# Gate and up products of a SwiGLU layer as seven half products instead of eight, in two token groups

## The reference, cut to what matters

```
def swiglu(hn, w_gate_up, w_down):
    gate, up = jnp.split(hn @ w_gate_up, 2, axis=-1)
    return (jax.nn.silu(gate) * up) @ w_down

        h = h + memory_cross_attention(hn, mem, ...)      # ends with  o @ w_xo
        hn = rmsnorm(h, norm_ffn_g[l])
        h = h + swiglu(hn, w_gate_up[l], w_down[l])
    return rmsnorm(h, norm_final_g)
```

## Time and profile before

| what | us |
|---|---|
| median of 3 runs (2631.83 to 2634.83) | 2632.27 |
| the profiled execution | 2631.12 |
| its span | 2629.4 |
| PE busy in the span | 2526.4 |
| DVE / ACT / POOL busy | 1284.7 / 546.5 / 283.7 |

### The profile page before, as it was taken

One profiled execution on the slowest core, in us unless ns is written; L12 is line 12 of the kernel. 1 busy time (PEld: TensorE's weight loads), 2 busy tenths in 40 slices (PEclk: granted clock), 3 DMA queues, 4 the chain that ended last, 5 costly groups with the idle time before them and its releaser, 6 DMA issues.

```text
span 2629.4 us, 31047 instructions
## 1 busy us (share of the span) xinstructions
PE 2526.4 (96%) x11282; PEld 2056.1 (78%) x11282; DVE 1284.7 (49%) x2113; ACT 546.5 (21%) x733; POOL 283.7 (11%) x238
## 2 busy tenths in 40 slices
PE   6899999799999999999999999999999999999994
PEld 4688887688888788888768888888888888888883
DVE  6634553368880784352442554434434434433437
ACT  5301110322221432130331321111111111111122
POOL 3278870000000220000000000000000000000001
PEclk9999999999999999999999999999999999999997
DMA  5432227532226642222310000000000000000002
GB/s 191 133 117 99 86 74 156 146 122 80 80 80 168 200 175 76 84 96 80 104 57 32 32 33 32 33 32 32 32 32 32 32 32 32 32 32 32 32 16 96
DMA packets 87288, 201.27 MB, mean 77 GB/s; under 512 B 12608, under 2 KB 41792, under 8 KB 87232
## 3 DMA queue, kind: packets, MB, share of 16 engines
q1 hardware_dynamic: 83872, 189.01, 22.2%
q0 software_dynamic: 3360, 11.54, 1.4%
HBM read 148.64 MB, written 53.97 MB: 77 GB/s over the span
## 4 chain that ended last, share of the span: by engine, by line
PE 90%; DVE 3%; DMA 2%; issue 2%; POOL 1%; ACT 1%; SPq 0%; DVEq 0%; POOLq 0%; ACTq 0%
PE bank L616 28%; PE bank L617 28%; PE bank L618 28%; PE bank L893 2%; PE bank L839 1%; PE bank L870 1%; DMA BBL<-scratch_BB 1%; POOL ACC L515 1%; DMA scratch_CO<-COS 1%; DVE HR L1774 1%; PE bank L836 0%; DVE ACC L1613 0%; PE bank L713 0%; PE bank L882 0%; PE bank L781 0%
## 5 line engine op out<-in xcount | busy, mean ns | idle before, releaser
L616 PE MATMUL bank<-XN,WLO 128*128 128x512 f32 x2400 | 935.5, 390 | 3.1 <-DVE XN L1711 1.7
L617 PE MATMUL bank<-XN,WHI 128*128 128x512 f32 x2400 | 933.8, 389 | 0.0
L618 PE MATMUL bank<-XN,WHI 128*128 128x512 f32 x2400 | 933.7, 389 | 0.0
L616 PEld LDWEIGHTS bank<-XN,WLO 128*128 128x128 f32 x2400 | 450.4, 188 | 98.8 <-issue 5.1
L617 PEld LDWEIGHTS bank<-XN,WHI 128*128 128x128 f32 x2400 | 450.5, 188 | 94.2 <-issue 1.0
L618 PEld LDWEIGHTS bank<-XN,WHI 128*128 128x128 f32 x2400 | 450.4, 188 | 93.9
L948 ACT ACTIVATE WHI<-WR 128x1024 fp32r<-128x1024 f32 x150 | 157.7, 1051 | 603.1 <-PE bank L618 537.3
L1243 DVE TENSOR_TENSOR WLO<-WR,WHI 128x1024 fp32r<-128x1024 f32 x150 | 197.8, 1319 | 126.3 <-ACT WHI L948 118.0
L1758 DVE TENSOR_TENSOR HR<-bank,HR 128x512 f32<-128x512 f32 x264 | 181.8, 691 | 126.9 <-PE bank L618 125.0
L616 PE MATMUL bank<-AF,WLO 128*128 128x512 f32 x528 | 208.2, 394 | 0.7 <-DVE HR L1758 0.7
L617 PE MATMUL bank<-AF,WHI 128*128 128x512 f32 x528 | 208.0, 394 | 0.0
(11 more groups left out here) (200 smaller groups left out, 2526.4 us busy)
## 6 DMA issues: line engine op xcount, KB each, us to landing
WR<-W_all SPq DMA_DIRECT2D x150, 512.0 KB, 3.3
scratch_G<-GS SPq DMA_DIRECT2D x16, 768.0 KB, 3.8
XS<-xT SPq DMA_DIRECT2D x8, 768.0 KB, 4.9
scratch_CO<-COS SPq DMA_DIRECT2D x8, 768.0 KB, 4.1
COL<-scratch_CO SPq DMA_DIRECT2D x8, 768.0 KB, 4.3
G2L<-scratch_G SPq DMA_DIRECT2D x8, 768.0 KB, 5.8
G1L<-scratch_G SPq DMA_DIRECT2D x8, 768.0 KB, 7.2
XR<-xT SPq DMA_DIRECT2D x8, 768.0 KB, 4.3
```

Of the source, the lines that this page charges most:

```text
L616: pe_mm(out, w[1], x[0], start=first, stop=False)
L617: pe_mm(out, w[0], x[1], start=False, stop=False)
L618: return pe_mm(out, w[0], x[0], start=False, stop=last)
```

## The change

The eight half products of a gate/up step (gate and up, two halves of the 1024 features, two halves of the tokens) become seven (Strassen's scheme in the form with four combinations on either side). Tokens are taken in two groups of 768 (`GRP`), each of two halves of 384 (`HB`); the whole feed-forward part runs once for each group, with all weights read twice. A step is one D_FF tile of one group: 7 products of 4 k tiles x 3 matmuls of 384 columns. A chunk's down part is 4 entries of 24 matmuls of 384 columns. A step's activations are gated during the next step (`gated`, `gated_lo`), so the down part of a chunk stands after the first step of the next one.

The weights now pass through an entry ring: an entry is 128x512, its high part made by ACT (`EH`), its low part by DVE (`EL`), six entries (`RINGF`) ahead of PE. Three of a step's seven entries come straight from the loaded slots (`RAW`, three buffers), four are combinations that GpSimd makes into `SW` (`combine`). The combinations of the inputs (`XF`, `XH`, `XL`) are made once for each group; as silu stands behind sums of products, the norm's reciprocal is now multiplied into the inputs. `XN` is no longer used after xo; `AF` moves from `w0` + 48 KB to `base` + 84 KB (`base` is 2048; `w0` is 133312, that is 64 bytes above a multiple of 128). Group 0's final norm is computed in group 1's first steps, its output written late in group 1's last chunks, and stored by SP after the last weight load.

```
+PRODUCTS = ((0, B11), (1, T2), (0, B21), (1, T3), (2, T1), (3, T4), (2, B22))
+    def operand(kind, rg, ru):
+        gate, up = RAW[rg % RAWS], RAW[ru % RAWS]
+        return (gate[:, 0:BLK], SW[1][:], gate[:, BLK:], SW[2][:], SW[0][:], up[:, BLK:], SW[3][:])[kind]
 # SP
-        with loop(nc.sync, (NSLOT - 2 - SLOT0["ffn"]) // 2) as i:
-            for par in range(2):
-                weights(SLOT0["ffn"] + par + 2, par, i)
+            def pair(i):
+                raw_load(r + 4, f0 + 6 + 6 * i, n + 7 + 18 * i)
+                raw_load(r + 5, f0 + 7 + 6 * i, n + 10 + 18 * i, G_STEPS * g + 2 + 2 * i)
+                raw_load(r + 6, f0 + 4 + 6 * i, n + 13 + 18 * i)
+                raw_load(r + 7, f0 + 5 + 6 * i, n + PAIR0 + 3 + 18 * i, G_STEPS * g + 3 + 2 * i)
+                raw_load(r + 8, f0 + 8 + 6 * i, n + PAIR0 + 6 + 18 * i)
+                raw_load(r + 9, f0 + 9 + 6 * i, n + PAIR0 + 9 + 18 * i)
 # GpSimd
+        def combine(s, rg, ru, i, read):
+            pool.wait_ge(S(f"raw{ru % RAWS}"), raw_count(ru, i))
+            if read is not None:
+                pool.wait_ge(S("entry_lo"), read)
+            nc.gpsimd.tensor_tensor(SW[0][:], up[:, 0:BLK], up[:, BLK:], ALU.add)
+            nc.gpsimd.tensor_tensor(SW[1][:], SW[0][:], gate[:, 0:BLK], ALU.subtract)
+            nc.gpsimd.tensor_tensor(SW[2][:], gate[:, 0:BLK], up[:, 0:BLK], ALU.subtract)
+            nc.gpsimd.tensor_tensor(SW[3][:], gate[:, BLK:], SW[1][:], ALU.subtract)
+            def pair(i):
+                combine(s + 2 + 2 * i, r + 4, r + 5, i, n + PAIR0 + 18 * i)
+                combine(s + 3 + 2 * i, r + 8, r + 9, i, n + PAIR0 + 7 + 18 * i)
 # PE
+        def ffn_step(n, p, s, g, first=False):
+            for j, (bk, op) in enumerate(PRODUCTS):
+                pe.wait_ge(S("entry_lo"), n + j + 1)
+                if first:
+                    pe.wait_ge(S("x_ready"), 7 * g + j + 1)
+                if j == 2:
+                    pe.wait_ge(S("first_kept"), s + 1)
+                if j == 3:
+                    pe.wait_ge(S("summed"), 5 * s + 1)
+                if j == 6:
+                    pe.wait_ge(S("summed"), 5 * s + 3)
+                for a in range(HT):
+                    last = product(PS[bk][:, 0:HB], ...)
+                last.then_inc(S("products"), 1)
+            def pair(i):
+                ffn_step(n + PAIR0 + 18 * i, 2, s + 2 + 2 * i, g)
+                down(n + PAIR0 + 7 + 18 * i, 3, d + i)
+                ffn_step(n + PAIR0 + 11 + 18 * i, 1, s + 3 + 2 * i, g)
 # ACT, in a step
+            for j in range(7):
+                act.wait_ge(S("products"), 7 * s + j + 1)
+                if j == 0:
+                    copy(S1T[:], PS[0][:, 0:HB]).then_inc(S("first_kept"), 1)
+                if j == 2:
+                    nc.scalar.activation(SG1[:], PS[0][:, 0:HB], ACT.Silu)
+                if j == 0:
+                    next_hi(6, n + 6, q, s, rg, ru, i)
+                elif follow == "S":
+                    next_hi(j - 1, n + 6 + j, q, s + 1, ng, nu, i)
+                elif j < 5:
+                    down_hi(j - 1, n + 6 + j, q, rd, i)
+                if j in (1, 2) and not fresh:
+                    act_hi(s - 1, 1 - odd, j - 1)
+                if j == 6:
+                    act.wait_ge(S("summed"), 5 * s + 5)
+                    nc.scalar.activation(SG2[:], G2T[:], ACT.Silu)
 # DVE, in a step
+            for j in range(7):
+                if j == 1: with_first(U2T, 1, S1T, ...)
+                if j == 3: with_first(U3T, 1, S1T, ...)
+                if j == 4: with_first(UP2, 2, U3T, ...)
+                if j == 5: with_first(UP1, 3, U3T, ...)
+                if j == 6: with_first(G2T, 2, U2T, ...)
+                (entry_lo of entry n + 6 + j)
+                if j in (1, 2) and not fresh:
+                    gated(s - 1, j - 1)
+                if j == 3 and not fresh:
+                    gated_lo(s - 1, 1 - odd, 0)
+                    gated_lo(s - 1, 1 - odd, 1)
 # DVE, ahead of group 0 (ahead of group 1 the same order, mixed with down_add of the last chunk)
-        residual("xo", 2, False)
+        norm_reciprocal(0)
+        norm_reciprocal(1)
+        normed(0, B11, 0, 0).then_inc(S("x_made"), 1)
+        then(normed(0, T3, 0, 1))
+        tt(xf(T1), xf(T3), xf(B11), ALU.subtract)
+        x_lo(0, 0)
+        then(normed(0, B22, 1, 1))
+        entry_lo(1, ...); entry_lo(2, ...)
+        V.tensor_tensor(xf(T2), xf(B22), xf(T1), ALU.subtract).then_inc(S("x_made"), 1)
+        normed(0, B21, 1, 0).then_inc(S("x_made"), 1)
+        tt(xf(T4), xf(B21), xf(T2), ALU.subtract)
+        x_lo(0, 1)
+        x_lo(0, 2)
+        V.tensor_tensor(xf(T3), xf(B22), xf(T3), ALU.subtract).then_inc(S("x_made"), 1)
+        entry_lo(3, ...); x_lo(0, 3); entry_lo(4, ...); x_lo(0, 4); entry_lo(5, ...); x_lo(0, 5); x_lo(0, 6)
+        norm_reciprocal(2)
+                if last and g:
+                    for k in range(KT):   # group 0's output, 8 operations of 768 columns
+                        V.scalar_tensor_tensor(out=h, in0=h, scalar=gains[:, 4, k:k + 1], in1=RB[:, 0:GRP], ...)
...
```

More of the change, by code:

```diff
@@ L945, in _ @@
+        final_sums(1)
     @block.scalar
@@ new lines, in down, with x_hi, final_square @@
+        def down(n, p, s, d, ng, nu, i):
+            for m in range(4):
+                act.wait_ge(S("down_made"), 16 * d + 4 * m + 4)
+                next_hi(2 + m, n + 6 + m, (p + 6 + m) % RINGF, s, ng, nu, i)
+        def x_hi(g, j):
+            act.wait_ge(S("x_made"), 4 * g + min(j + 1, 4))
+            copy(XH[j][:], XF[j][:]).then_inc(S("x_high"), 1)
+        def final_square(g, k, out):
+            act.wait_ge(S("down_added"), 16 * (CHUNKS * (g + 1) - 1) + 2 * (k + 1))
+            if g == 0 and k:
+                act.wait_ge(S("final_added"), k)
+            nc.scalar.activation(out[:], HR[:, k, g * GRP:(g + 1) * GRP], ACT.Square).then_inc(S("final_squares"), 1)
@@ L1763, in _, with xo_pair @@
[L1763 to L1771 removed]
+        then(V.memset(ACC2[:], 0.0))
+        def xo_pair(i):
+            for par in range(2):
+                j = 2 * i + par
+                if not (isinstance(i, int) and i == 3 and par):
+                    lo(SLOT0["xo"] + par + 1, 2 * i)
+                for b in range(NB):
+                    h = one(HR, j)[:, blk(b)]
+                    V.tensor_tensor(h, take(RES0["xo"] + NB * par + b, i, 2 * NB), h, ALU.add).then_inc(evac, 1)
+                if par or not (isinstance(i, int) and i == 0):
+                    add_squares(2, j - 1, SQ2[:, 1 - par, :])
@@ new lines, in down_add, with down, normed @@
+        def down_add(d, g, m):
+            for r in range(4):
+                dve.wait_ge(S("down_made"), 16 * d + 4 * m + r + 1)
+                h = HR[:, 2 * m + r // 2, gcol(g, r % 2)]
+                V.tensor_tensor(h, PS[4 + r][:, 0:HB], h, ALU.add).then_inc(S("down_added"), 1)
+        def down(n, p, s, d, g, ng, nu, i):
+            for m in range(4):
+                down_add(d, g, m)
+                next_lo(2 + m, n + 6 + m, (p + 6 + m) % RINGF, s, ng, nu, i)
+        def normed(g, out, half, b):
+            for a in range(HT):
+                k = half * HT + a
+                last = V.scalar_tensor_tensor(out=XF[out][:, a, :], in0=HR[:, k, gcol(g, b)],
+                                              scalar=gains[:, 3, k:k + 1], in1=RB[:, gcol(g, b)],
+                                              op0=ALU.mult, op1=ALU.mult)
+            return last
```

516 lines of the change are left out of this document (379 added, 137 removed).

## The result

The changed kernel takes 2669.93 us (median; 2667.18 to 2670.76) where the kernel before took 2632.05 beside it: a ratio of 1.0141, 95% interval 1.0123 to 1.0158, so it is slower by 38 us, where I had forecast 11. The direction came out as forecast and the time lies inside the range, but the change is more than three times the forecast one: the forecast was 27 us too low, because the stalls of TensorE cost more than I had priced them at.

The account below looks back on a forecast made before the run. PE, busy 96% of the span, was taken as the bound: 1495.9 + 1006.6 + 42 + 22 + 5 + 4.3 + 1.7 + 40 + 23.9 = 2641.4 us of span, so 2643 forecast, range 2600 to 2682.

Parts of the forecast that it names:

- Distance of matmuls (173.3 ns): Feed-forward part on PE: each 384-column matmul costs 173.3 ns, 5808 of them 1006.6 us, a gain of 81.
- the columns' case (170.0): Rival, feed-forward matmuls: the surplus goes by columns, 170.0 ns each, minus 19 us, 2624; chance 0.13.
- the weight loads (188): Rival, feed-forward matmuls: a weight load of 188 ns bounds each one, 1091.9 us, no gain, 2728; chance 0.03.
- AF's surplus: Down matmuls: AF's 20.0 ns surplus is 6.7 larger from starting 64 bytes off; aligned like XN, down costs 173.3.
- GpSimd and DVE take turns: Steps beside combine: their times add, delaying a step's third sum; PE stalls 2.0 in 20 steps, 40 us (to 52).
- The rival in which the four operations fall into DVE's waits for ACT: Inside steps: GpSimd costs little, a step loses 0.3 instead of 2.0, 34 us go, 2609; chance 0.23.
- Between the groups, 22 + 5 + 2: PE waits 22 us for activations and group 1's inputs, 5 for group 0's norm, about 2 for a step's stall.
- Output operations, 4.3: Group 0's eight 768-column output operations on DVE stand before a down part; PE waits 4.3 us.
- Way in 42: From xo to the first steps: inputs need the norm first, step 0 ends at 1552.2 not 1510.5, 42 us lost.
- tail 23.9: Behind the last matmul: 23.9 us instead of 42.1, a gain of 18, as half the tokens are already out.
- the last down part: End of group 1: PE waits 1.7 us again for the activations gated only then.
- late chain: Rival, inside steps: handovers take 0.2 more, all 44 steps lose 0.8 more, plus 35 us, 2678; chance 0.14.

Follow-up runs that it names:

- b1_aligned: The kernel before with the region of AF, YHL, CIN and MN starting at a multiple of 128 bytes instead of 64; 2614.31 us, ratio 0.9931.
- e1_pool16: The changed kernel with GpSimd's four weight combinations of a step only 16 columns wide, except in step 0, so most combination work is left out; 2615.23 us.
- e2_early: The changed kernel with the first three of GpSimd's four combinations of a step started two entries earlier, nothing left out; 2637.00 us, ratio 1.0015.
- b2_aligned: The kernel before with four tiles' region at a multiple of 128 bytes, run again on e8_again's chip; 2613.89 us, ratio 0.9921.
- e8_again: Repeat of the changed kernel with early combinations (not group 0's step 1), spread output operations, inputs 3 to 6 in the first step, 128-byte region; 2609.96 us.
- e5_inter: The changed kernel with x_hi and x_lo of inputs 3 to 6 made inside a group's first step instead of ahead of it; 2666.74 us, ratio 1.0127.
- e4_inputs4: The changed kernel with group 1's inputs made only 4 columns wide per tile, so most of their combinations are left out, every wait kept; 2650.01 us.
- e3_spread: The changed kernel with group 0's eight output operations spread over a down part and the last step instead of one block; 2660.71 us, ratio 1.0110.

## Why the direction was right and the size was wrong

**Distance of matmuls (173.3 ns): right.** In the trace of after the distances under 200 ns have a mean of 173.4 and a median of 173 with AF moving (2030 of them), 173.6 and 173 with XH or XL (3502). The surplus over 2.4 GHz is 13.3 ns for each matmul, at 384 as at 512 columns; the columns' case (170.0) and the weight loads (188) are out. By the formula that the Trainium skill, TensorE: Matmul & The Clock Gate, section Back-to-back issue gap, gives for the isolated gap, it would have been an estimated 162.5; the trace disagrees for fp32r (173.3).

**AF's surplus: right.** I gave down 173.3 because its new place is aligned like XN. b1_aligned shows that this is the cause.

**GpSimd and DVE take turns: right, and the place of the stall too.** Forecast 2.0 in each of 20 steps; the idle records of those 20 sum to 39.0 us (42.1 in 22, the other two, 1.2 and 2.0, stand in steps 22 and 24). e1_pool16 and e2_early show that it is the turns inside the step. The Trainium skill, SBUF — State Buffer, section Who interferes with whom, calls it a lock that lets the second wait until the first is done; L2019's 1.64 us agrees. The rival in which the four operations fall into DVE's waits for ACT, which I gave 0.23, is refuted as the kernel stood; it is what e2_early makes of it.

**The step that failed: what a stall costs TensorE.** Inside the steps I took 20 x 2.0 = 40, a stall at full clock and nothing behind it. TensorE loses 2.2 by the stall, counted from start to start, as the matmuls of 1806.87 to 1809.42 show, and that is all such a step loses (16.77 - 14.56 = 2.21). And in 4 steps a fall to half the clock follows, 1.57 each, for which the sum had nothing. The 19 steps outside the stretch between the groups lose 2.17 on average without the half clock: 19 x 2.17 + 4 x 1.57 = 47.5 of the 49.9 lost in three rows of the table (steps 1 to 21, 25 to 41, and 41), where I had 38. The 16 steps between them give the rest, 0.14 each at their own length of 31.34. I had counted the half clock only in the way in, after an idle of 8.44. Yet the trace of before has a short stall of this kind, outside the feed-forward part: near the start PE stands idle for 2.32 us at full clock, and 0.8 us after it goes on the clock falls to 1.2 GHz for some 3.4 us. A stall of 1.68 us at 1365.11 has no such fall behind it. The stall and a window behind it:

```profile
71.29 0.50 PE L616 MATMUL bank<-MN,WLO 128*128 128x512 f32 x1 [2.32 <-DVE WLO L1243]
...
72.30:75.60 3.30, 3.30 (x9) 2.55 (x8) 1.83 (x2) 1.11 (x2) 2.70 (x1) 0.50 0.78 307
```

So the rows for this price were there before the forecast. e1_pool16's gain of 54.7, against 42.1 us of waits that went, shows it from the other side.

**Between the groups, 22 + 5 + 2: measured 36.3.** The order of the waits was as worked out (AF, HR three times, S1T, U2T, UP), but their sum was not what I had too low. Up to the start of step 23 the idle records give 17.7 where I had 22: AF 3.5 for 1.7, HR 7.4 for 9.9, S1T 2.5 for 5.3, U2T 3.1 for 3.6, UP 1.2 for 1.5. The stretch still loses 26.2, because the starts behind the seven stalls come 1.1 later than the idle time says and some 40 matmuls behind four of them start 320 ns apart, some 6 us more. Group 0's sums and the stall of step 23, 5 + 2, took 10.1, about 1.6 of it at half clock. AF's chain (copy, silu, gate, copy, split) is as long at the end of a group as inside a step, and I had let it end sooner.

**Output operations, 4.3: measured 10.3.** The block took 8.54 instead of 7.0. Its first operation took 2.03, since GpSimd was at work from 2587.38 to 2589.11, and the other seven follow 0.93 apart, not 0.88:

```profile
2587.38 1.73 POOL L688 TENSOR_TENSOR SW<-RAW,SW 128x512 f32<-128x512 f32 x1
L2150 DVE SCALAR_TENSOR_TENSOR HR<-HR,gains,RB x8: 1004/1005/2033, 2587.9 to 2595.4; 128x768 f32<-128x768 f32 x8
```

It began late, at 2587.89, since the entry ahead of it in DVE's order waited for ACT's copy, and that copy for GpSimd; in e1_pool16 PE's gap here is 5.28 us instead of 7.61. And 16 matmuls behind the gap ran at half clock, 2.3 us. I had priced a block by its length over the time of the part ahead, and not asked what DVE waits for before it.

**Way in 42 and tail 23.9: right** (44 and 24.6). Products 0 to 3 were due at 1516.3, 1526.8, 1538.5 and 1543.9 and started at 1518.40, 1529.21, 1540.17 and 1545.78: late by 1.7 to 2.4, and the error does not grow from product to product. With half the tokens in it the tail costs 17.5 us less, as worked out.

**The bias.** Seven terms of the sum came out larger and one smaller (the last down part, 1.3 for 1.7). Apart from the start at xo's end (0.6, inside the scatter of that stretch) they were chains of single durations at full clock with the smallest handover between them. I had put the excess only into a rival (0.8 in all 44 steps, late chain, 0.14), which is not where it was: 0.2 in the steps with a stall, 0.14 in the others of the pairs, and half clock behind stalls. The forecast of 2643 has a slip of its own: 2641.4 with both surcharges, 1.7 and 1.2, is 2644.3.

## What to carry to other kernels

Before arithmetic is traded for operations on another engine, work out the chain inside one step and not the busy share: DVE at 61% and GpSimd at 20% cost PE 42 us of waits here and the kernel 54.7, because four of their turns fell into the one stretch without slack. The same operations two entries earlier cost 0.32 a step instead of 2.2. Price a new stall above the idle time that a trace shows for it: an idle of 1.93 us was 2.2 from start to start, and 4 times in 19 a stretch at half clock followed that cost 1.57. And read the matmul distance by moving tile first: 6.7 ns between two tiles in one kernel was worth 19.5 us by one rounding constant (b2_aligned), of the 23.4 that the best version of the change reached with it on the same chip (e8_again).

## What the runs showed of the hardware

- An fp32r matmul with a moving tile at a multiple of 128 bytes: 226.7 ns at 512 columns (before, b1_aligned) and 173.3 at 384 (after), so 13.3 above the columns at 2.4 GHz. With a tile 64 bytes off: 6.7 more (AF, YHL and CIN 233.3 to 226.7 by the address alone).
- Weight loads of 188 to 192 ns in the records do not bound matmuls 173 apart.
- GpSimd and DVE, each with two operands in SBUF, alternate in the trace of after: DVE's 0.55 becomes up to 1.64, GpSimd's 1.29 becomes 1.61. DVE's operations with one operand in a bank (L2012, 176 of them) take 0.54 to 0.56 throughout.
- A stall of 1.93 us at full clock (2.32 in before, at 71.29) can be followed by some 3.4 us at 1.2 GHz: in 4 of the 19 steps with such a stall outside the stretch between the groups in the traces of after and e5_inter, in 2 of them in e4_inputs4 and e3_spread, in none of the same steps in e1_pool16 and e2_early, which have no such stall. What chooses the steps stays open.
- The idle time in the records is shorter than the loss: 1.93 us idle stand between starts 2.27 apart instead of 0.17, and the next start comes 0.11 late (after, 1806.87 to 1809.42).
